# A transformer pair of layers on one core: one split of weights in eight goes behind the first halves of its block

## The reference

```python
o = m @ w_out                                     # first layer's output projection
x = x + gate * rms_norm(o, post_gain)
...
h = h + nsa_mixer(rms_norm_2(h, norm_mix), ...)
hn = rms_norm_2(h, norm_ffn)
h = h + jnp.square(jax.nn.relu(hn @ ffn_w1)) @ ffn_w2      # 2048 -> 8192 -> 2048
gate = jax.nn.sigmoid(rms_norm_2(h, norm_ple) @ ple_w_gate)
h = h + (p @ ple_w_proj) * gate
return rms_norm_2(h, norm_final)
```

## Time and profile before

| | us |
|---|---|
| median of 3 runs | 2226.84 |
| lowest, highest | 2225.49, 2227.36 |
| profiled execution | 2229.68 |
| its span, first to last instruction | 2228.0 |

### The profile page before, as it was taken

The page is one execution under the profiler, slowest core; times in us unless marked ns, Lnnn a source line. Parts: engine busy times, 40 slices in busy tenths (PEclk is TensorE's granted clock), DMA queues, the critical chain, the costliest instruction groups (busy, mean ns, idle before and its releaser), DMA issues.

```text
span 2228.0 us, 40905 instructions
## 1 busy us (share of the span) xinstructions
PE 2184.8 (98%) x15336; PEld 1883.8 (85%) x15336; DVE 1565.3 (70%) x2398; ACT 1107.5 (50%) x1749; POOL 105.2 (5%) x96
## 2 busy tenths in 40 slices
PE   6999999999999999999999999999999999999997
PEld 5998888888888888888888878888888888888887
DVE  6975877888887587677666668665565565566767
ACT  3444645555554465465444545544444454445454
POOL 0000000000000010200000002000000000000202
PEclk8999999999999999999999999999999999999999
DMA  9995455445545576565544336455555555555552
GB/s 364 406 373 180 161 176 167 159 164 171 170 163 170 171 262 229 179 204 187 174 133 142 132 124 211 167 197 187 183 178 191 186 179 188 185 182 182 186 180 85
DMA packets 116273, 424.88 MB, mean 191 GB/s; under 512 B 13232, under 2 KB 13616, under 8 KB 115888
## 3 DMA queue, kind: packets, MB, share of 16 engines
q1 hardware_dynamic: 111744, 406.61, 54.1%
q0 software_dynamic: 4400, 16.45, 2.2%
HBM read 414.62 MB, written 8.39 MB: 190 GB/s over the span
## 4 chain that ended last, share of the span: by engine, by line
PE 88%; DVE 7%; ACT 2%; issue 2%; DMA 1%; SPq 0%; DVEq 0%; POOL 0%; ACTq 0%
PE ps L2181 46%; PE ps L2182 22%; PE ps L2288 5%; PE ps L2557 2%; DVE wlo L1311 2%; PE ps L2230 1%; PE ps L2231 1%; PE ps L2232 1%; DVE acc L1342 1%; PE ps L2558 1%; ACT whi L725 1%; PE ps L2710 1%; DVE pr L1965 1%; DMA xt<-in_x 0%; PE ps L2254 0%
## 5 line engine op out<-in xcount | busy, mean ns | idle before, releaser
L2181 PE MATMUL ps<-acts,whi 128*128 128x512 f32 x3312 | 1205.4, 406 | 3.2 <-DVE wt L1317 1.7
L1311 DVE TENSOR_TENSOR wlo<-raw,whi 128x1024 fp32r<-128x1024 f32 x629 | 786.1, 1259 | 557.2 <-ACT whi L725 554.5
L725 ACT ACTIVATE whi<-raw 128x1024 fp32r<-128x1024 f32 x671 | 703.7, 1057 | 690.2 <-PE ps L2182 604.3
L2182 PE MATMUL ps<-acts,wlo 128*128 128x256 f32 x3312 | 928.4, 280 | 0.0
L2181 PEld LDWEIGHTS ps<-acts,whi 128*128 128x128 f32 x3312 | 621.7, 188 | 165.8 <-issue 8.3
L2182 PEld LDWEIGHTS ps<-acts,wlo 128*128 128x128 f32 x3312 | 625.6, 189 | 4.6 <-issue 3.4
L2181 PE MATMUL ps<-hidn,whi 128*128 128x512 f32 x1280 | 455.0, 400 | 2.2 <-DVE s L1317 1.7
L2182 PE MATMUL ps<-hidn,wlo 128*128 128x256 f32 x1280 | 358.2, 280 | 0.0
L2181 PEld LDWEIGHTS ps<-hidn,whi 128*128 128x128 f32 x1280 | 240.3, 188 | 66.3 <-DVE s L1317 4.1
L2182 PEld LDWEIGHTS ps<-hidn,wlo 128*128 128x128 f32 x1280 | 241.4, 189 | 0.5 <-issue 0.5
L725 ACT ACTIVATE half<-ps 128x256 f32<-128x256 f32 (+1 forms) x335 | 125.9, 382 | 66.0 <-PE ps L2182 50.6
(11 more groups left out here) (341 smaller groups left out, 2004.3 us busy)
## 6 DMA issues: line engine op xcount, KB each, us to landing
raw<-in_stream SPq DMA_DIRECT2D x767, 512.0 KB, 4.2
gate_dram<-stage POOLq DMA_DIRECT2D x32, 128.0 KB, 2.5
gab<-gate_dram POOLq DMA_DIRECT2D x8, 512.0 KB, 5.3
xt<-in_x SPq DMA_DIRECT2D x1, 2048.0 KB, 9.7
xt<-in_x POOLq DMA_DIRECT2D x1, 2048.0 KB, 8.7
ple_dram<-pr__111 POOLq DMA_DIRECT2D x4, 512.0 KB, 3.7
pj<-ple_dram POOLq DMA_DIRECT2D x1, 2048.0 KB, 11.8
out<-y__143 SPq DMA_DIRECT2D x2, 512.0 KB, 2.8
```

Source lines behind the costliest of these rows:

```text
L725: return nc.scalar.activation(dst, src, ACT.Copy)
L1311: tt(wlo[:, n % SPLIT, :], raw[:, in_stream(g) % RAW, :], whi[:, n % SPLIT, :].bitcast(F32), ALU.subtract).then_inc(raw_used, 1)
L2181: mm(ps[bank + n][:, :], whi[:, n0 % SPLIT, c:c + P], act[:, off + kt + k, :], start=kt + k == 0, stop=False)
L2182: ins = mm(ps[bank + n][:, 0:T], wlo[:, n0 % SPLIT, c:c + P], act[:, off + kt + k, 0:T], start=False, stop=kt + k == last)
```

## The change

In the four places named above, VectorE's split for j = 7 (the block's eighth place, the tile that TensorE needs as the third of the next block) moves from ahead of the four first halves to behind them. ScalarE, TensorE, GpSimd and SP are left as they are, and no semaphore changes. The block that mixes the two branches and the attention stages keep the old order.

```diff
             with dve.Fori(0, 4) as b:
-                for j in range(8):
+                for j in range(7):
                     split(WO0 + j + AHEAD, b)
                 for n in range(4):
                     first_half(tile_of(ob, b * 4 + n), n, E + n, b * 4)
+                split(WO0 + 7 + AHEAD, b)
...
             def scaled_block(g0, e, dst, b, first):
-                for j in range(8):
+                for j in range(7):
                     split(g0 + j + AHEAD, b)
...
                 for n in range(4):
                     first_half(dst(n), n, e + n, b * 4)
+                split(g0 + 7 + AHEAD, b)
                 for n in range(4):
                     dve.wait_ge(evac_done, b * 4 + (e + n + 1))
                     tt(dst(n), dst(n), rs[:, :], ALU.mult).then_inc(s.scaled, 1)
...
             def relu_block(f, b, i, first):
-                for j in range(8):
+                for j in range(7):
                     split(FF0 + j + AHEAD, i)
...
                 for n in range(4):
                     first_half(s4[:, n, :], n, E + n, i * 4)
+                split(FF0 + 7 + AHEAD, i)
...
             def down(f):
...
-                    for j in range(8):
+                    for j in range(7):
                         split(FF0 + 32 + j + AHEAD, i)
                     for n in range(4):
                         first_half(s4[:, n, :], n, E + 16 + n, i * 4)
+                    split(FF0 + 32 + 7 + AHEAD, i)
...
             for b in range(4):
-                for j in range(8):
+                for j in range(7):
                     split(g0 + j + AHEAD)
...
                 for n in range(4):
                     first_half(s4[:, n, :], n, e + n)
+                split(g0 + 7 + AHEAD)
```

## The result

| | before, us | after, us |
|---|---|---|
| median of 20 runs | 2226.43 | 2210.60 |
| lowest, highest | 2223.72, 2230.19 | 2208.00, 2225.02 |
| profiled execution | 2229.68 | 2210.12 |
| its span | 2228.0 | 2208.4 |

The ratio is 0.9939, with a 95% interval of 0.9928 to 0.9950: faster by 0.5 to 0.7%. Forecast were 2221.1 and a range of 2206.5 to 2224.5. The median hides the form of the result: **the times after the change fall into two groups**, 15 of 20 at 2208.0 to 2211.8 and 5 at 2222.5 to 2225.0, with nothing between. The times before form one group. The lower group holds the median; the forecast of 2221.1 lies between the two groups, where no run fell.

What follows compares the result with a forecast made beforehand. TensorE was taken as the bound (88% of the chain). Gains of 1.8 (projection), 3.8 (feed-forward) and 0.5 us (last gate), together 6.1, less 0.4 for the last block, gave 5.7 off 2226.8: 2221.1 us, range 2206.5 to 2224.5.

Steps and rivals of the forecast that it cites:

- The stall and what ends it: At changed block boundaries, TensorE's wait of 0.13 us for VectorE's first halves and 0.10 restart go wholly.
- The rival that the return of the loop keeps part of the stall: At changed boundaries, the stall is only partly or not at all VectorE's: 2224 or 2226.8 us; chance 0.18.
- Two spacings, held without disturbance: TensorE's matmul pairs take 0.3467 or 0.3533 us each, and the spacing changes, if at all, at a boundary's stall.
- The two cases that the prediction told apart by the spacing: Feed-forward part slow throughout, 2221.1 us (chance 0.50 as worked out), or fast throughout, 2208 (rival, chance 0.17).
- the rival that hung on the rule, 2219.0: In all changed blocks, each keeps its present spacing and only stalls are gained, 7.8 us; chance 0.09.
- Which spacing is drawn: In the feed-forward part, the slow spacing that follows the sum of squares in its first block lasts: 0.3533 us a pair.
- the fast part: Rival: the feed-forward part's pairs stay at 0.3467 us, a further 13.1 us gained, 2208; chance 0.17.
- the feed-forward part's 3.8 us: Feed-forward part: 1,985 spacings at 0.3533 us take 701.3 instead of 705.1 us, a gain of 3.8.
- 8 fast blocks turning slow: In the changed stages, 8 fast blocks becoming slow give back 3.4 us of the 8.2 us gained from stalls.
- The projection: Output projection: 192 spacings stay fast at 0.3467 us, 66.6 instead of 68.4 us, a gain of 1.8.
- The delay behind the halves: Work behind the first halves starts 1.14 us later; the tightest lead at the fourth tile shrinks from 1.75 to 0.4, costing nothing.
- The last block: At the last block's seventh tile, a new wait of 0 to 1.2 us for a split or copy, taken as 0.4.

Runs made afterwards that it cites:

- e10: Kernel before, VectorE's old order kept, with only TensorE's four matmuls a quarter reordered to high, high, low, low: 2219.64 us beside 2228.72, ratio 0.9959.
- e8: Changed kernel with a quarter's four matmuls in the order high, high, low, low instead of alternating: 2210.57 us beside 2225.46 for the kernel before, ratio 0.9933.
- e3: Changed kernel with the old order kept in the four blocks of the first down pass: 2222.41 us beside 2231.66 for the kernel before, ratio 0.9962.
- e7: Changed kernel with the same move also in the attention stages and the attention's output projection: 2213.5 us beside 2231.8 for the kernel before, ratio 0.9926.
- e4: Changed kernel unaltered, run again: 2223.01 us beside 2231.66 for the kernel before, ratio 0.9944; 4 of 10 runs in the lower group.
- e9: Changed kernel unaltered, run once more: 2209.63 us beside 2225.46 for the kernel before, ratio 0.9946; 9 of 12 runs in the lower group.
- e2: New order in output projection and last gate only, feed-forward part as in the kernel before: 2228.13 us beside 2231.66 for the kernel before, ratio 0.9989.
- e5: Changed kernel with a second split (j = 6) also behind the halves throughout the feed-forward part: 2232.2 us beside 2231.8 for the kernel before, ratio 0.9999.

## Why the prediction was right, and where it wasn't

**The stall and what ends it.** Right, with its numbers: no wait of TensorE for a first half is left, the first half comes 0.7 us ahead (0.65 forecast), and the waits and restarts sum to some 9 us in e10 (8.2 forecast for the old order of matmuls). The rival that the return of the loop keeps part of the stall is out: 2,046 pairs pass 31 boundaries without a late one.

**Two spacings, held without disturbance.** Right, and it decides the result. The two cases that the prediction told apart by the spacing are the two groups that were measured, though its figures lie at or below their lower edges: 2208 where 2208.0 to 2211.8 was measured, 2221.1 where it was 2222.5 to 2225.0. A fixed cost per matmul (the Trainium skill, TensorE: Matmul & The Clock Gate, Wait — 56ns, not 53.3ns?) would give one spacing. The trace of e8 has one, with high, high, low, low, but not of that size: by the Trainium skill's figures a pair would take 0.325 us (an estimate: 768 columns at 2.4 GHz and 2.5 ns twice), and it took 0.3485. The alternation has two, and the rival that hung on the rule, 2219.0, did not occur.

**Which spacing is drawn: the step that failed.** The prediction said that behind the sums of squares the slow one follows, ten times of ten, and lasts. It lasts, but 28 of 42 executions had the time of the fast one, and the profiled one is fast through the whole part, which the prediction itself named as a sign that it is wrong. The ten restarts were ten of one execution. In the trace before, the pairs ahead of all ten have the slow spacing too. In the trace after, the pairs ahead of the sum of squares are already fast and stay so behind it; over the ten traces with this order of matmuls the sum of squares in the first feed-forward block kept the spacing ahead of it in all but one (e3, slow before, fast behind). So the ten were no independent draws but mostly one spacing carried on. What the prediction left out is the step into the part, near 1390 us, where TensorE waits in nine of the ten traces (not in e7): there the spacing turned from slow to fast in the profiled run after, in e4 and in e9, and from fast to slow in e3. The chance of 0.17 for the fast part was far too low.

**The range and luck.** The term that failed is the feed-forward part's 3.8 us, 1,985 pairs taken at 0.3533. The same span gained 17.0 us in the profiled run (705.1 to 688.1), at 0.3466. The median of 2210.60 lies 10.5 us below the forecast and in the range only because the range took in most of the rival. Which group holds the median was itself a matter of chance: the same kernel's median was 2223.01 in e4 and 2209.63 in e9.

**The sum against the median.** Against the profiled execution it gave 2224.0; the upper group's middle time is 2223.9 in the first runs. Subtracting 5.7 from the median gave 2221.1, below every run of that group. The profiled execution before took 2229.68 with 7 fast blocks of 31; e2's had 17 and took 2222.25. Likely the median execution had more fast blocks than the profiled one, and so more to lose by all turning slow; it has no trace. The term "8 fast blocks turning slow" was sized from one execution. (A slip besides: the chances of the times below 2222.4 add up to 0.43 + 0.17 + 0.09 = 0.69, not 0.68.)

**The projection** was taken to stay fast. In the profiled run after, it is slow from the waits of its first tile on (869 us), and gains 0.2 us instead of 1.8. In e4 and e9 it is fast throughout. So it is the same kind of draw, at those waits.

**The delay behind the halves.** Right to 0.15 us: leads of 0.27 to 0.8 us at the fourth tile where 0.4 was forecast for the tightest, and no wait. e5 shows that it passes through once for each split moved: behind the first blocks of the down pass, where the part is fast in both traces, the lead at the fourth tile is 3.67 us in the trace after and 2.53 in e5's, 1.14 less. And the limit was near: twice the delay costs all that the change gains.

**The last block.** A new wait was forecast between 0 and 1.2 us, taken as 0.4. It is there, at the seventh tile:

```profile
2177.69 3.48 DVE L1311 TENSOR_TENSOR wlo<-raw,whi 128x1024 fp32r<-128x1024 f32 x3
...
2183.24 2.51 DVE L2152 TENSOR_TENSOR xt<-xt,q 128x256 f32<-128x256 f32 x1
2187.58 2.36 DVE L1311 TENSOR_TENSOR wlo<-raw,whi 128x1024 fp32r<-128x1024 f32 x2 [1.83 <-ACT whi L725]
...
2188.72 0.28 PE L2801 MATMUL ps<-acts,wlo 128*128 128x256 f32 x1
2188.86 0.39 PE L2799 MATMUL ps<-acts,whi 128*128 128x256 f32 x1
2189.08 0.28 PE L2800 MATMUL ps<-acts,whi 128*128 128x256 f32 x1
```

Two starts, 2188.86 and 2189.08, are late by 0.02 and 0.10 where the others follow by 0.12: 0.12 us in all. As expected the three splits now follow each other without a gap (3.48 us where the earlier trace rows had 5.19), and beside GpSimd's squares the product and the addition take long instead (1.22 and 2.51 us, where the next quarter's take 0.43 each). The upper end of 1.2 us that the meeting with the squares might have cost did not come.

## What to carry to other kernels

Put what a later block waits for ahead of what has slack, but count the slack of everything that the moved step delays: here one split fitted with 0.27 us to spare, and a second one cost the whole gain. A kernel whose times fall into two groups is judged group by group, from the trace, and not by a median of a few runs. And a count of ten from one trace may be one event seen ten times.

## What the runs showed of the hardware

With a long and a short matmul in alternation (512 and 256 columns, fp32), TensorE held one of two spacings at the same granted clock (1.00), 0.3467 or 0.3533 us a pair, for 700 us on end, and in the stages followed here changed between them only where it had waited or done something else. Such a disturbance may change it and may not; in the two traces of the old order 7 and 17 of 31 blocks were fast. With both long matmuls first there was one spacing, 0.3485 a pair. What decides a draw stays open: granted clock and TensorE's busy time were the same in fast and slow traces, runs of one kernel fell into both groups, and no experiment set the spacing at will. Nor is it shown why the order high, high, low, low has no second spacing.

A wait for a semaphore costs more than its length: 0.13 us of wait at a boundary brought 0.1 us of restart. A lead of 0.27 us, on the other hand, cost nothing.
